# Token-stationary products with 128x128 transposes in the second pair of layers of a four-layer network

## What is computed

```
layer 0:  z = x @ w_in                      (1024 -> 2048: q, k, v, u of 512 columns each)
          8 heads of stick-breaking attention on q, k, v
          a state-space scan over the tokens on u, then a gated linear unit
          x = layer_norm(ALPHA * x + both @ w_out)
          x = layer_norm(ALPHA * x + square(relu(x @ w1)) @ w2)        w1: 1024 x 4096
layer 1:  z = x @ w_in                      (q, k, v and a small index part)
          index scores choose the keys that a token sees; 16 heads of softmax attention
          x = layer_norm(ALPHA * x + heads @ w_out)
          x = layer_norm(ALPHA * x + square(relu(x @ w1)) @ w2)
```

## Time and profile before

| what | value |
|---|---|
| median of 3 runs | 3764.23 us |
| lowest, highest | 3763.64, 3775.64 us |
| the profiled execution's own time | 3755.99 us |
| its span, first to last instruction | 3754.7 us |
| mean granted clock of PE | 0.84 of 2.4 GHz |
| PE / DVE / ACT / POOL busy | 72% / 53% / 19% / 41% |
| DMA, mean | 305 GB/s |

### The profile page before, as it was taken

The page is one execution under the profiler, slowest core; times in us unless marked ns, Lnnn a source line. Parts: engine busy times, 40 slices in busy tenths (PEclk is TensorE's granted clock), DMA queues, the critical chain, the costliest instruction groups (busy, mean ns, idle before and its releaser), DMA issues.

```text
span 3754.7 us, 35721 instructions
## 1 busy us (share of the span) xinstructions
PE 2697.8 (72%) x12920; PEld 1223.2 (33%) x12920; DVE 2004.3 (53%) x5005; ACT 722.9 (19%) x1792; POOL 1540.9 (41%) x1632
## 2 busy tenths in 40 slices
PE   7758787787556775656697476565555499999998
PEld 2213332211112321111343121111114395766755
DVE  1156577745767677875213667777745655122311
ACT  0012212211122322211311121121112121020200
POOL 0034565554776666777100367767752000000000
PEclk9869988799877887776898687768887699999999
DMA  8578898899999999999432699999985268476657
GB/s 290 192 269 297 325 368 333 334 399 397 409 409 350 381 397 372 368 409 409 150 118 79 262 355 409 409 363 409 409 339 213 90 239 288 163 281 218 248 199 260
DMA packets 357508, 1145.99 MB, mean 305 GB/s; under 512 B 33412, under 2 KB 33668, under 8 KB 356308
## 3 DMA queue, kind: packets, MB, share of 16 engines
q0 software_dynamic: 236256, 867.34, 59.9%
q1 hardware_dynamic: 120660, 276.13, 20.5%
q10 hardware_dynamic: 416, 0.23, 0.0%
HBM read 1142.43 MB, written 1.15 MB: 305 GB/s over the span
## 4 chain that ended last, share of the span: by engine, by line
PE 45%; DMA 24%; DVE 17%; ACT 5%; POOL 5%; issue 3%; SPq 0%; DVEq 0%; ACTq 0%; POOLq 0%
DMA BIG<-in_p_u_dram,IDX 11%; PE PS L1012 9%; PE PS L1078 8%; DMA BIG<-in_p_v_dram,IDX 7%; DVE BIG L1873 6%; PE PS L1301 6%; PE PS L1283 5%; POOL BIG L2250 4%; DMA WR<-in_w_mod_dram 3%; PE PS L977 3%; PE PS L1040 2%; PE PS L1178 2%; PE PS L1272 2%; PE PS L988 1%; ACT dg L1468 1%
## 5 line engine op out<-in xcount | busy, mean ns | idle before, releaser
L1078 PE MATMUL PS<-BIG,dg 64*64 64x512 f32 x6144 | 1005.0, 784 | 669.0 <-DMA BIG<-in_p_v_dram,IDX 424.5
L2250 POOL DMA_INDIRECT BIG<-in_p_u_dram,IDX x768 | 737.7, 961 | 980.1 <-ACT PS L1455 463.1
L1873 DVE CUSTOM_DVE_ANT_0 BIG<-BIG,PS 128x1024 f32<-128x1024 f32 x768 | 930.3, 1216 | 322.3 <-DMA BIG<-in_p_u_dram,IDX 317.2
L2250 POOL DMA_INDIRECT BIG<-in_p_v_dram,IDX x768 | 734.3, 956 | 307.6 <-issue 136.0
L1078 PEld LDWEIGHTS PS<-BIG,dg 64*64 64x64 f32 x6144 | 263.0, 164 | 1327.9 <-issue 854.3
L1012 PE MATMUL PS<-WR,HT 128*128 128x512 f32 x640 | 300.9, 623 | 11.4 <-DMA WR<-in_b_w_in_dram 6.1
L1468 ACT ACTIVATE dg<-twin,ACTV 128x64 f32<-128x64 f32 x768 | 207.9, 336 | 330.0 <-PE PS L1078 220.7
L1283 PE MATMUL PS<-HT,WR 128*128 128x128 f32 x2048 | 258.3, 287 | 8.4 <-DMA WR<-in_mlp_w_dram 5.0
L1283 PEld LDWEIGHTS PS<-HT,WR 128*128 128x128 f32 x2048 | 248.1, 201 | 18.0 <-issue 6.2
L1301 PE MATMUL PS<-WR,BIG 128*128 128x512 f32 x512 | 227.3, 598 | 0.0
L977 PE MATMUL PS<-WR,scS 128*2 128x512 f32 x384 | 179.1, 620 | 38.9 <-DMA WR<-in_w_mod_dram 38.6
(11 more groups left out here) (295 smaller groups left out, 2730.8 us busy)
## 6 DMA issues: line engine op xcount, KB each, us to landing
WR<-in_mlp_w_dram SPq DMA_DIRECT2D x128, 1024.0 KB, 6.1
WR<-in_w_mod_dram SPq DMA_DIRECT2D x48, 1024.0 KB, 11.1
WR<-in_b_w_in_dram SPq DMA_DIRECT2D x18, 1024.0 KB, 9.6
WR<-in_a_w_in_dram SPq DMA_DIRECT2D x16, 1024.0 KB, 11.0
WR<-in_p_w_q_dram SPq DMA_DIRECT2D x16, 1024.0 KB, 9.4
BIG<-in_sb_ssm_w_in_dram POOLq DMA_DIRECT2D x16, 1024.0 KB, 7.5
BIG<-in_dsa_w_dram POOLq DMA_DIRECT2D x16, 1024.0 KB, 8.2
BIG<-in_p_u_dram,IDX POOLq DMA_INDIRECT x768, 9.4
```

The lines of the kernel that those rows point to most:

```text
L1078: mm = self.e.matmul(pv[64 * i:64 * i + 64, 2 * r + n, :], dg[p, :], row[p, n * 512:n * 512 + 512], start=h == 0 and j == 0, stop=h == 7 a ...
L1873: self.e.tensor_tensor_reduce(row, row, xp, 1.0, 0.0, ALU.mult, ALU.add, m.ACTV[:, u % 4, j:j + 1]).then_inc(*self.done("dot", l, u, j))
L2250: self.e.indirect_dma_start(row, None, m.A[f"p_{table}"], bass.IndirectOffsetOnAxis(ap=m.IDX[:, u % 4, j:j + 1], axis=0)).then_inc(*m.GR.l ...
```

## The change

All products of a block that moved the 128 tokens now keep the tokens in the array and move up to 512 columns of weights. The result has tokens on the partitions, so it is copied to SBUF and transposed in 128x128 pieces.

- `up` makes half a slab's contraction (4 matmuls of 512 columns) per beat, 16 beats in all, and gives each 1 MB half back at once. ACT takes the relu into SBUF, DVE multiplies it with the PSUM values (relu times x is relu squared), and `up_turn` transposes the 512 columns in four pieces, which ACT copies into F. It comes one slab later, after the second half; the last one stands by itself ahead of `down`.
- `down_begin` and `down` wait for ACT's copies; UP now has four banks, which include DOWN's two.
- `columns` goes: u, q, k and the three of `dsa_project` use `rows_of` and then `turn` (four transposes, a copy on ACT). `turn` follows one beat later for u and in `dsa_project`, and behind the next product for q and k.
- `dsa_index` makes 512 and 136 columns, and `index_turn` (three transposes, two copies) follows one beat later.

```diff
@@ Chip.__init__
-        self.UP = Slots([PSt[:, 4 + i, :] for i in range(2)])
+        self.UP = Slots([PSt[:, 4 + i, :] for i in range(4)])
+        self.RT = Slots([self.tmp[:, i, :] for i in range(2)])
@@ sb
-        self.columns(u, 4, self.block_of(b), m.s_u, after)
+        self.rows_of(u, self.block_of(b), None, after)
         if b == 0:
             self.coefficients()
         self.side_slab(q, w, 0)
+        yield
+        self.turn(u, m.s_u)
         yield
@@ attention
-        self.columns(q, 4, self.block_of(b), m.a_q, ())
+        self.rows_of(q, self.block_of(b), None, ())
         self.side_slab(v, w, 1024)
         yield
-        self.columns(k, 4, self.block_of(b), m.a_k[:, :, b * 128:(b + 1) * 128], ())
+        self.rows_of(k, self.block_of(b), None, ())
+        self.turn(q, m.a_q)
...
-        self.rows_of(v, self.block_of(b), m.a_v[:, :, b, :])
+        self.rows_of(v, self.block_of(b), m.a_v[:, :, b, :], ())
+        self.turn(k, m.a_k[:, :, b * 128:(b + 1) * 128])
@@ mlp
-            for j in range(4):
-                self.up(l, b, n, j, after)
-                if n and j == 1:
-                    self.square(l, b, n - 1)
+            for half in range(2):
+                self.up(l, b, n, half, after)
+                if n and half:
+                    self.up_turn(l, b, n - 1)
                 yield
-        self.square(l, b, 7)
+        self.up_turn(l, b, 7)
@@ dsa
         self.dsa_index(b)
+        yield
+        self.index_turn(b)
         yield
@@ dsa_project
-            self.columns(("dsa", b, n), 4, self.block_of(b), dst, ())
+            self.rows_of(("dsa", b, n), self.block_of(b), None, ())
+            yield
+            self.turn(("dsa", b, n), dst)
             yield
@@ Tensor
+    def turn(self, slab, dst):
+        m = self.m
+        ps, rows = m.PS.take("turn", slab), m.RT.of(slab)
+        self.wait_ge(m.act.at("rows", slab), *m.PS.emptied("turn", slab))
+        for i in range(4):
+            mm = self.e.transpose(ps[:, i * 128:(i + 1) * 128], rows[:, i * 128:(i + 1) * 128], m.ident[:, :])
+        mm.then_inc(*self.done("turn", slab))
+        m.RT.free((slab,), self.done.last())
...
-    def up(self, l, b, n, j, after):
+    def up(self, l, b, n, half, after):
         m, slab = self.m, ("w1", l, b, n)
-        ps = m.UP.of(l, b, n) if j else m.UP.take(l, b, n)
-        self.wait_ge(*after, *m.UP.emptied(l, b, n))
-        for k in range(8):
-            self.wait_ge(m.W.landed(slab, k // 4))
-            mm = self.e.matmul(ps[:, j * 128:(j + 1) * 128], m.slab_of(slab, k // 4)[:, k % 4, j * 128:(j + 1) * 128],
-                               m.HT[:, k, 256:384], start=k == 0, stop=k == 7)
-        mm.then_inc(*self.done("up", l, b, n, j))
-        if j == 3:
-            for k in range(2):
-                m.W.free((slab, k), self.done.last())
+        ps = m.UP.of("up", l, b, n) if half else m.UP.take("up", l, b, n)
+        self.wait_ge(*after, *m.UP.emptied("up", l, b, n), m.W.landed(slab, half))
+        for k in range(4):
+            mm = self.e.matmul(ps, m.HT[:, 4 * half + k, 256:384], m.slab_of(slab, half)[:, k, :],
+                               start=half == 0 and k == 0, stop=half == 1 and k == 3)
+        mm.then_inc(*self.done("up", l, b, n, half))
+        m.W.free((slab, half), self.done.last())
+
+    def up_turn(self, l, b, n):
+        m = self.m
+        ps, rows = m.UP.take("turn", l, b, n), m.RM.of(l, b, n)
+        self.wait_ge(m.dve.at("up", l, b, n), *m.UP.emptied("turn", l, b, n))
+        for i in range(4):
+            mm = self.e.transpose(ps[:, i * 128:(i + 1) * 128], rows[:, i * 128:(i + 1) * 128], m.ident[:, :])
+        mm.then_inc(*self.done("up turn", l, b, n))
+        m.RM.free((l, b, n), self.done.last())
...
-        self.wait_ge(*m.DOWN.emptied(l, b))
+        self.wait_ge(*m.DOWN.emptied(l, b), m.act.at("square", l, b, 7))
...
-        self.wait_ge(m.dve.at("square", l, b, k // 4), m.W.landed("w2", l, b, k))
+        self.wait_ge(m.act.at("square", l, b, k // 4), m.W.landed("w2", l, b, k))
@@ Scalar
+    def turn(self, slab, dst):
+        m = self.m
+        self.wait_ge(m.pe.at("turn", slab))
+        self.e.activation(dst, m.PS.of("turn", slab).rearrange("p (i t) -> p i t", i=4), ACT.Copy).then_inc(
+            *self.done("turned", slab))
+        m.PS.free(("turn", slab), self.done.last())
...
+    def up(self, l, b, n, half, after):
+        m = self.m
+        if half:
+            row = m.RM.take(l, b, n)
+            self.wait_ge(m.pe.at("up", l, b, n, 1), *m.RM.emptied(l, b, n))
+            self.e.activation(row, m.UP.of("up", l, b, n), ACT.Relu).then_inc(*self.done("relu", l, b, n))
+
+    def up_turn(self, l, b, n):
+        m = self.m
+        self.wait_ge(m.pe.at("up turn", l, b, n))
+        self.e.activation(m.F[:, 4 * n:4 * n + 4, :], m.UP.of("turn", l, b, n).rearrange("p (f t) -> p f t", f=4),
+                          ACT.Copy).then_inc(*self.done("square", l, b, n))
+        m.UP.free(("turn", l, b, n), self.done.last())
@@ Vector
+    def up(self, l, b, n, half, after):
+        m = self.m
+        if half:
+            row = m.RM.of(l, b, n)
+            self.wait_ge(m.act.at("relu", l, b, n), m.pe.at("up", l, b, n, 1))
+            self.e.tensor_tensor(row, row, m.UP.of("up", l, b, n), ALU.mult).then_inc(*self.done("up", l, b, n))
+            m.UP.free(("up", l, b, n), self.done.last())
```

More of the change, by code:

```diff
@@ L326 @@
     intra = inter = read_state = group_norm = group_scale = group_gate = tail_begin = coefficients = drive = nothing
-    power = local_scan = carry_scan = spread_scan = columns = rows_of = side_half = side_one = nothing
+    power = local_scan = carry_scan = spread_scan = turn = rows_of = side_half = side_one = nothing
     sb_scores = sb_logs = sb_beta = sb_sums = sb_weights = sb_outs = ssm_read = glu = sb_gate = out = nothing
-    norm_block = up = square = load_w2 = down_begin = down = mlp_out = dsa_begin = dsa_index = nothing
+    norm_block = up = up_turn = index_turn = load_w2 = down_begin = down = mlp_out = dsa_begin = dsa_index = nothing
     index_heads = score_mask = score_top = score_bias = dsa_products = dsa_scores = dsa_spread = dsa_outs = end = nothing
@@ L1168, in inter, with rows_of @@
                       skip_group_check=True).then_inc(*self.done("inter", h, j, n))
[L1170 to L1175, removed]
-            for k in range(8):
-                self.wait_ge(m.WB.landed(slab, k // 4))
-                mm = self.e.matmul(ps[:, i * 128:(i + 1) * 128], self.side_of(slab, k)[:, i * 128:(i + 1) * 128], rhs(k),
-                                   start=k == 0, stop=k == 7)
-        mm.then_inc(*self.done("cols", slab))
-        for k in range(2):
-            m.WB.free((slab, k), self.done.last())
     def side_of(self, slab, k, n=512):
         return cut(self.m.WB.of(slab, k // 4), 4, cols=n)[:, k % 4, :]
-    def rows_of(self, slab, lhs, dst):
+    def rows_of(self, slab, lhs, dst, after):
         m = self.m
         ps = m.PS.take("rows", slab)
-        self.wait_ge(*m.PS.emptied("rows", slab))
+        self.wait_ge(*after, *m.PS.emptied("rows", slab))
         for k in range(8):
@@ L1357, in dsa_outs @@
         ps, pt = m.PS.take("o", b, h), m.PT.of(b, h)
[L1358 removed]
+        self.wait_ge(m.act.at("p", b, h), m.act.at("index", b), *m.PS.emptied("o", b, h))
         for sk in range(b + 1):
@@ L1624, in norm_block @@
         self.norm((tag, b), None, b)
-    def square(self, l, b, n):
+    def up(self, l, b, n, half, after):
         m = self.m
-        rl = m.RM.take(l, b, n)
-        self.wait_ge(m.pe.at("up", l, b, n, 3), *m.RM.emptied(l, b, n))
-        self.e.activation(rl, m.UP.of(l, b, n), ACT.Relu).then_inc(*self.done("relu", l, b, n))
-        m.UP.free((l, b, n), self.done.last())
+        if half:
+            row = m.RM.take(l, b, n)
+            self.wait_ge(m.pe.at("up", l, b, n, 1), *m.RM.emptied(l, b, n))
+            self.e.activation(row, m.UP.of("up", l, b, n), ACT.Relu).then_inc(*self.done("relu", l, b, n))
@@ L1638, in dsa_index @@
-        self.e.activation(m.d_ki[:, b * 128:(b + 1) * 128], ps[:, 256:384], ACT.Copy).then_inc(*self.done())
-        m.PS.free(("di", b), self.done.last())
-        ps = m.PS.of("dv", b)
-        self.wait_ge(m.pe.at("dv", b))
-        self.e.activation(m.d_wi, ps[:, 256:264], ACT.Copy).then_inc(*self.done())
-        self.e.activation(m.d_v[:, b, :], ps[:, 0:256], ACT.Copy).then_inc(*self.done("dsa in", b))
-        m.PS.free(("dv", b), self.done.last())
+        ps, row = m.PS.of("index", ("dsa_v", b)), m.RT.take("index", b)
@@ new lines, in dsa_index @@
+        self.wait_ge(m.pe.at("index", ("dsa_v", b)), *m.RT.emptied("index", b))
+        self.e.activation(row[:, 0:256], ps[:, 256:512], ACT.Copy).then_inc(*self.done())
+        self.e.activation(m.d_v[:, b, :], ps[:, 0:256], ACT.Copy).then_inc(*self.done())
+        m.PS.free(("index", ("dsa_v", b)), self.done.last())
+        ps = m.PS.of("index", ("dsa_i", b))
```

(10 more changed lines are left out.)

68 lines of the change are left out of this document (27 added, 41 removed).

## The result

The changed kernel takes **3813.7 us** (median of 4 runs, 3810.6 to 3818.1), the kernel before 3766.5 (4 runs, 3763.6 to 3775.6): ratio **1.0124** with a 95% interval of 1.0106 to 1.0142, so 47 us or 1.2% slower. The forecast was 3803 (3781 to 3832).

A forecast was written before the change was run, and what follows sets the result against it. The tail was taken as bound by PE's queue, busy 91% to 95% in four stretches. Terms -2 + 21.8 + 7.5 + 8.7 + 3.3 = +39 us gave 3795 on the profiled execution, 3803 as median; range 3781 to 3832.

The forecast's parts named there:

- The mechanism that it held decisive: Beats: up takes 16, not 32, so the MLP ends with beat 32; mixer work on DVE behind it loses cover.
- Arithmetic: PE's prices: +0.17 us per w1 slab, +1.4 per MLP; mixer products +0.5 a step; dsa_index -1.4 a step.
- rival of wide instructions at 0.40 of the narrow ones' time: Wide matmuls at 0.18 us each for 0.43, four MLPs at -34 us; about 3630 us; chance 0.01.
- Second stretch: MLP beside sb(1): 14 scans, output and norm exposed behind the last down; +21.8 us, bounds +14 to +32.
- Third and fourth stretch: MLPs beside dsa: heads exposed behind the last down, w1 waits gone; +7.5 and +8.7 us, bounds 0 and +18 each.
- POOL's loads wait for the same products: Transfers stay 1 MB each and in order, and POOL's loads wait for the same products; no cost was given.
- Last stretch: Last MLP alone: arithmetic 1.4 and hand-over 1.9 give +3.3 us, bounds 1.5 to 5.
- gap of 1.9 us: Hand-over from up to down: uncovered wait for the last turn and ACT's copy, 1.9 us per MLP, bounds 0.8 to 2.7.
- First stretch: Mixer of block 0 alone: u and k gain behind their transfers, against turns and copies; -2 us, bounds -5 to +2.
- the cover is not needed: Rival: DVE's leftover mixer work behind beat 33 runs beside a PE still behind with matmuls; 3748 us, chance 0.07.
- Exposure at the low clock: Rival: heads at 2.4 and 3.5 us, scans' 32, no stall gone; 3833 us, chance 0.10.

The follow-up runs named there:

- e2: Changed kernel with mlp_out and the norm held back 18 beats beside sb and 9 beside dsa; 3786.3 us, ratio 1.0053.
- e4: Changed kernel with dsa_project's next load issued right behind the product that empties its buffer, ahead of the turn; 3798.6 us, ratio 1.0096.
- e3: Changed kernel with up in 32 beats of 2 wide matmuls each; 3780.2 us, ratio 1.0040.
- e6: Changed kernel with two of sb(1)'s local and spread scans per beat instead of one; 3789.5 us, ratio 1.0058.
- e5: Changed kernel with the last up_turn behind the first down and its transposes in other PSUM banks; 3807.0 us, ratio 1.0104.
- e1: Kernel before, narrow matmuls kept, with up in 16 beats; 3794.0 us, ratio 1.0080.
- e9: Kernel before, narrow matmuls, with 16 beats of up, two scans per beat, mlp_out held back 9 and 8 beats; ratio 0.9934 on a slower chip.
- e11: Kernel before, narrow matmuls, 16 beats of up, two scans per beat, mlp_out held back, rerun on another chip; 3741.5 us, ratio 0.9932.

## Why the prediction was right

The mechanism that it held decisive was the right one, and the sum landed 11 us short of the measured median, inside the range. That it came so near is in part luck: one term failed and another was too small, and some that no run isolates were too dear.

- *Arithmetic.* Slab 6.87 + 0.44, index product 8.72 for 8.8, `up` never waits for a w1 slab: as priced. The rival of wide instructions at 0.40 of the narrow ones' time fell: the trace has 6.87 us for 16 wide instructions against 7.15 for 64 narrow ones, 0.96. The Trainium skill ("TensorE: Matmul & The Clock Gate", Back-to-back issue gap) gives 131 ns for 512 columns against 81 for 128, from which the 0.40 is an estimate; the measurement decides against it here.
- *Second stretch.* Forecast: 165.5 to the last `down`, 35.2 of DVE's work, 36.8 from the read-out, 237.5 in all. Measured: 165, 35.0 and 35.6, 235.7. The terms hold; of the reason only half did (e2): the scans are bound to the last `down` by PE's queue as well as by `mlp_out`.
- *Third and fourth stretch.* Forecast +7.5 and +8.7, measured +12.8 and +13.8. Two terms were off. The step "POOL's loads wait for the same products" failed: e4 gives 8.4 and 5.1 us for it. And from the last `down` to the first `out` it took 20.5 and 27.1 us by these windows of after, not 18.0 and 23.1. The granted clock was 0.50 while PE worked at the heads, and a head took 1.75 and 2.82 us, where 1.5 and 2.3 had been taken, nearer to DVE's pace. Together these two terms exceed the 5.3 and 5.1 us by which the stretches missed, by some 6 and 4; which terms were too dear for it stays open.

```profile
3411.50:3432.00 20.50, 13.04 (x41) 6.82 (x41) 14.05 (x44) 10.74 (x34) 0.00 (x0) 0.62 0.16 52
```

```profile
3633.60:3660.70 27.10, 19.96 (x71) 11.13 (x71) 16.99 (x44) 12.39 (x35) 0.00 (x0) 0.62 0.12 39
```

- *Last stretch.* Forecast +3.3, measured +5.3. The gap of 1.9 us was about right: from the end of the last product at 3744.53 to the first `down` at 3747.28 it is 2.75, less two turns of 0.44. e3, e4 and e6, with the same code there, take 129.8 and 129.9, so 2.4 and 2.5 above before, and e2 3.5. The term stands. What after has beyond e4 and e6, 2.8, is 1.7 of slow clock in its profiled execution (see e5) and 1.1 in the first two slabs.
- *First stretch.* Forecast -2, measured +1.2 by windows. The part that was priced, u and k behind their transfers, is there: the scores start 3.7 us earlier after block 0's flip than before. It was given back on POOL, where one mask took 18.20 us instead of 11.73; see the last section. Where that mask took 12 us or less, the stretch took 172.3 to 174.2 us with narrow products and 170.3 and 170.4 with wide ones; where it took about 18, 180.4 (e1) and 175.4 to 176.7. Like compared with like, the form gains 2 to 5 us, but the comparison rests on few executions.

Of the rivals, "the cover is not needed" fell with the result, which has the idle time, and with e1, which has it without any other part of the change. "Exposure at the low clock" was right about the clock and about the heads' direction. It was wrong about sizes (heads at 2.4 and 3.5 us, scans 32 us; measured 1.75 and 2.82, and 35.0 with output and norm) and about stalls: the wait for the w1 slab did go.

## What to carry to other kernels

When two chains share in-order queues by beats, the beats are the schedule. Halving one chain's count moves everything of it to the front, and whatever of the other chain is left behind its end has no cover. Before changing a form, list for each queue (the DMA-issuing ones too) what stands in front of each instruction before and after; here that list holds the scans, the heads and the load behind the mask, which are most of the loss. And try the new order on the old form first: it may be worth more than the form.

## What the runs showed of the hardware

**A mask on POOL beside a busy DVE.** The same 128x512 affine_select takes 0.65 to 0.78 us in most places, and 18.20 in the first stretch of after, where DVE has tensor_tensor operations between SBUF tiles without a pause. Timelines of before, of after and of e4:

```profile
2895.98 11.73 POOL L2290 TENSOR_SCALAR_AFFINE_SELECT H<-H 128x512 f32<-128x512 f32 x1 [7.29 <-ACT H L1601]
```

```profile
2898.06 18.20 POOL L2320 TENSOR_SCALAR_AFFINE_SELECT H<-H 128x512 f32<-128x512 f32 x1 [7.30 <-ACT H L1615]
```

```profile
2901.28 5.61 POOL L2322 TENSOR_SCALAR_AFFINE_SELECT H<-H 128x512 f32<-128x512 f32 x1 [7.29 <-ACT H L1617]
```

e2 and e9 have 1.51 us, e11 11.74, and the others 17.9 to 18.2. Up to 12 us it costs nothing: e9 and e11 have the same code there, and both first stretches took 172.3 us. At 18 it costs: in the wide kernels 175.4 to 176.7 us instead of 170.3 and 170.4, in the narrow ones 180.4 (e1) instead of 172.3 to 174.2. In after the mask ends 0.4 us behind the last operation of DVE's series. In before, e2, e4, e6, e9 and e11 it ends together with one operation in the series, which took 0.75 to 0.78 us where its neighbours took 0.34 to 0.41. The Trainium skill ("SBUF — State Buffer", Who interferes with whom) says that a DVE instruction with two SBUF inputs contends with a GpSimd instruction that reads SBUF. The trace agrees in kind, with 18.20 us for 0.65; what lets the mask in early in one execution and at the end in another, in code that is the same, was not tried.

**Short waits and the clock.** The hand-over leaves PE two waits of 0.97 and 0.69 us, with 1.34 us of work in the three us around them. In after they were followed by 4 us at a granted clock of 0.57; before them it was 1.00. In e6, with the same waits, it stayed at 1.00. Windows of after, then of e6:

```profile
3744.30:3747.30 3.00, 1.34 (x10) 0.80 (x8) 0.69 (x1) 1.68 (x3) 0.00 (x0) 1.00 0.81 291
3747.30:3751.30 4.00, 4.00 (x6) 1.70 (x7) 0.00 (x0) 0.00 (x0) 0.00 (x0) 0.57 0.38 156
```

```profile
3720.30:3723.30 3.00, 1.34 (x10) 0.86 (x8) 0.69 (x1) 1.68 (x3) 0.00 (x0) 1.00 0.83 302
3723.30:3727.30 4.00, 4.00 (x10) 1.85 (x11) 0.00 (x0) 0.00 (x0) 0.00 (x0) 1.00 0.37 148
```

e2, e3 and e4 went like e6. So such waits can be followed by a slow clock, at 1.7 us here, and in four of five executions were not. What decides it no run shows. From after's trace alone the waits would have passed for its cause.
